# Convolution of prompt tiles 1 to 3 moved from VectorE to ScalarE and TensorE, with consumers of gathers queued later and 80 value rows fetched ahead

## Chip, cores and metric

The kernel runs on one core of a Trainium2 chip. The metric is the device time of one execution in microseconds (us), as the median of several runs. Times in the text that are places (such as "from 433 to 519") count from the start of the profiled span.

## What is computed

One layer of a hybrid decoder step: 512 prompt tokens in four tiles of 128, and 32 sample tokens (8 sequences of 4). Per token: a projection of x to 5192 columns, a gated causal depthwise convolution of width 31 over 512 channels, attention over keys that an indexer selects, a gated merge with an output product and layer norm, and then a product-key mixture of experts, in which each token takes 128 rows of a table `peer_u` and 128 rows of a table `peer_v` (16384 rows of 1024 floats each). Cut to what matters:

```python
u, q, k, v, qi, ki, wi, g_conv, g_attn = project_inputs(x, pos, w_in)   # u = a * sigmoid(b)
full = concatenate([prev, u])                                           # 30 rows of the past, then u
y = sum(full[n + k] * conv_w[k] for k in range(31)) + conv_b            # per channel, 512 channels
conv = silu(layer_norm(y)) @ w_conv_out
o = sparse_attend(q, k, v, select_keys(indexer_scores(qi, wi, ki), topk=128))
m = sigmoid(g_conv) * conv + sigmoid(g_attn) * o
h = layer_norm(ALPHA * x + m @ w_out)
idx, g = product_key_top16_of_8_heads(h @ w_query)                      # 128 experts per token
a = gelu(sum(h * peer_u[idx], -1)) * g
y = layer_norm(ALPHA * h + sum(a * peer_v[idx]))
```

Everything is float32.

## The kernel before

There are five tiles: 0 to 3 of the prompt, 4 for the samples. Each goes through a **front** (projection rows in, rotation, index scores, top-k, attention, convolution, merge, output product, layer norm, queries, routing) and then through the **mixer**: 128 gathers of u rows (tile 4: 32), each 128 partitions by 1024 floats (512 KB), each dotted with h on VectorE (L1908); Gelu and gates; then one gather of v rows per token (128, or 32 for tile 4), whose product with the weights TensorE sums into `acc` (L1552, in pairs; ScalarE first writes the weights of four tokens into a column, L1138). All gathers are issued by GpSimd (L800) in one list, `FETCHES`, which `fetches()` writes (L383 to L403). They land in `rings`: 5 slots for u, 6 for v. A gather waits until its slot is free, which is when the dot (semaphore `dotted`) or the product (`summed`) of the row before it in that slot is done. The first u gather of a tile also waits for the tile's first routed head (`routed`, L1716), and so on every 16.

The order of work on each engine is fixed when the program is built. Every piece of a front yields a number; the tables `CLOCK_0`, `CLOCK_1` and `CLOCK_T` turn it into a time of a planner's clock, fetches and their consumers have such times too (`fetches`, `uses`), and `merge` writes each engine's instructions in order of these times. So the clock only sets an order; on the chip, each engine goes through its own list and stops at each wait. Tile 0's u gathers stand at 176 and on, its first 64 v gathers (`EARLY_V`) at 470 and on, and from `MIXED_FROM` = 600 there are steps of 358.4 of the clock: step t holds the u gathers of tile t, the remaining v gathers of tile t-1 (first 24 u with two v each, then the rest spread), and the first 32 v of tile t. The consumer of a gather stands `LANDING` = 8 after it (14 for the first 32 v rows). The front of tile t+1 stands 103 after the start of step t.

The convolution works on `uT` (L113), the transposed gated rows with 30 columns of the past ahead. `taps` (L1730 to L1747) runs it on VectorE: for each of the 31 taps, four operations (one for each 128 channels) add a shifted view times the tap's weight into `conv_acc`. In tiles 1 to 3 it is merged with `attention` (L1806), between 0.195 and 0.475; attention itself runs from AT_ATT = 0.20 to AT_TAIL = 0.48, ahead of it the top-k from 0.09. An attention group is one or two heads: scores on TensorE (L1386), row maximum on VectorE (L1761), exp on ScalarE (L975), transposes on TensorE (L1403), their copy on ScalarE (L990), P·V on TensorE (L1415) into `wide`, heads 0 to 7 in its first bank and 8 to 15 in its second. Tile 1 has 8 groups, tiles 2 and 3 have 16. Then TensorE transposes the convolution's result after `conv_done` (L1261), ScalarE applies Silu (L929), and the products follow (L1243, queries L1304).

`wide` is free from the output product of the tile before until the first P·V; for tile 1, it is in use by the projection of all later tiles until `z_copied_b` has its last count.

## Time and profile before

| | us |
|---|---|
| median of 3 runs | 2325.19 (2320.65 to 2331.3) |
| profiled execution | 2312.72 |
| its span | 2310.9 |
| PE / DVE / ACT / POOL busy | 1513.1 / 1463.2 / 286.4 / 1251.1 |
| mean granted clock of TensorE | 0.789 |
| moved by DMA | 683.98 MB, 296 GB/s over the span |

A float32 product shows as two MATMUL records, a dot as two DVE records (the operation and the read of its accumulator). No engine is busy throughout, so the stretches have to be read one by one.

### The profile page before, as it was taken

How to read it: one execution, taken by the hardware profiler on the slowest of the kernel's cores; microseconds unless marked ns; L12 is line 12 of the kernel's file. 1: busy time of each engine (PE TensorE's matmuls, PEld its weight loads, DVE VectorE, ACT ScalarE, POOL GpSimd, SP SyncE). 2: the span in 40 equal slices, each digit the busy share in tenths (PEclk: the TensorE clock that was granted, in tenths of full speed). 3: DMA queues.
4: the chain of work that ended last, by engine and by line, in shares of the span. 5: the costliest groups of instructions: out<-in, count | busy, mean ns of one | idle time of the engine just before them, and what ended most of it. 6: DMA issues, size and time to landing. Idle time of an engine off the chain costs nothing.

```text
span 2310.9 us, 19606 instructions
## 1 busy us (share of the span) xinstructions
PE 1513.1 (65%) x6002; PEld 619.2 (27%) x6002; DVE 1463.2 (63%) x3807; ACT 286.4 (12%) x713; POOL 1251.1 (54%) x1108
## 2 busy tenths in 40 slices
PE   7889999268755356685546787556832887584244
PEld 3454444232411123231112334111100333141011
DVE  4319956971297899738589965776799641138431
ACT  1411102120101112010111211011100121000000
POOL 1003455654377667647677865777655644233654
PEclk9999999569977655798876878887555789777668
DMA  8807999868589888879998998999977999656996
GB/s 314 319 24 282 323 381 332 270 223 285 200 320 375 312 273 305 315 256 364 365 354 301 327 352 286 358 346 328 358 262 247 330 339 323 247 161 224 296 325 239
DMA packets 215683, 683.98 MB, mean 296 GB/s; under 512 B 27637, under 2 KB 63061, under 8 KB 208979
## 3 DMA queue, kind: packets, MB, share of 16 engines
q0 software_dynamic: 157376, 581.67, 71.0%
q1 hardware_dynamic: 51195, 91.90, 11.5%
q10 hardware_dynamic: 7008, 9.17, 1.1%
q8 instruction: 48, 0.79, 0.1%
q14 instruction: 56, 0.46, 0.1%
HBM read 669.97 MB, written 13.10 MB: 296 GB/s over the span
## 4 chain that ended last, share of the span: by engine, by line
DVE 31%; PE 28%; DMA 16%; POOL 13%; issue 8%; ACT 2%; SPq 2%; POOLq 0%; DVEq 0%; ACTq 0%
POOL rings L800 13%; DVE rings L1908 10%; PE acc L1552 9%; DMA rings<-peer_v,late 9%; DMA rings<-peer_u,late 5%; PE wide L1243 4%; DVE conv_acc L1744 3%; PE bank L1304 3%; DVE small L1616 2%; DVE uah L1619 2%; PE acc L1192 2%; DVE soft_score L1619 1%; PE wide L1464 1%; PE acc L1225 1%; PE bank L1456 1%
## 5 line engine op out<-in xcount | busy, mean ns | idle before, releaser
L1552 PE MATMUL acc<-rings,z_stages 128*32 128x512 f32 x2048 | 614.9, 757 | 499.7 <-DMA rings<-peer_v,late 303.1
L800 POOL DMA_INDIRECT rings<-peer_u,late x544 | 650.8, 1196 | 513.0 <-DVE late L1908 274.7
L800 POOL DMA_INDIRECT rings<-peer_v,late x544 | 591.6, 1088 | 446.9 <-PE acc L1552 295.9
L1908 DVE CUSTOM_DVE_ANT_0 rings<-rings,uah 128x1024 f32<-128x1024 f32 x288 | 348.9, 1223 | 149.5 <-DMA rings<-peer_u,late 145.4
L1908 DVE CUSTOM_DVE_ANT_0 rings<-rings,late 128x1024 f32<-128x1024 f32 x256 | 310.2, 1222 | 93.2 <-DMA rings<-peer_u,late 89.3
L1552 PEld LDWEIGHTS acc<-rings,z_stages 128*32 128x32 f32 x2048 | 126.4, 126 | 900.6 <-issue 897.1
L1225 PE MATMUL acc<-rings 128*128 128x512 f32 (+1 forms) x352 | 149.9, 578 | 0.0
L1744 DVE SCALAR_TENSOR_TENSOR conv_acc<-uah,conv_p,conv_acc 128x128 f32<-128x128 f32 x480 | 133.1, 347 | 0.0
L1678 DVE MAX8 uah<-zt 128x8 f32<-128x128 f32 (+1 forms) x80 | 22.7, 284 | 142.1 <-ACT zt L958 142.1
L1415 PE MATMUL wide<-keep,soft_score 128*128 128x64 f32 x320 | 62.0, 353 | 67.4 <-ACT soft_score L990 67.4
L1138 ACT COPY z_stages<-late 128x4 f32<-128x4 f32 x136 | 26.2, 198 | 574.7 <-PE acc L1552 507.7
L1304 PEld LDWEIGHTS bank<-uah,w_query_s 128*128 128x128 f32 x640 | 82.4, 210 | 25.1 <-issue 22.0
L1304 PE MATMUL bank<-uah,w_query_s 128*128 128x128 f32 (+1 forms) x640 | 87.2, 297 | 2.3 <-ACT uah L947 2.3
L1415 PEld LDWEIGHTS wide<-keep,soft_score 128*128 128x128 f32 x320 | 55.0, 258 | 104.3 <-ACT soft_score L990 96.9
L1225 PEld LDWEIGHTS acc<-rings 128*128 128x128 f32 x352 | 63.5, 193 | 71.2 <-issue 70.9
L1243 PE MATMUL wide<-w_out_s,uah 128*128 128x512 f32 (+1 forms) x160 | 79.0, 645 | 2.1 <-ACT uah L940 2.1
L1192 PE MATMUL acc<-rings 128*128 128x512 f32 (+2 forms) x176 | 69.2, 541 | 15.1 <-DMA small<-quarter 12.6
L1225 PE MATMUL wide<-rings,uah 128*128 128x512 f32 (+1 forms) x176 | 74.4, 565 | 0.0
L975 ACT ACTIVATE soft_score<-soft_score,small 128x128 f32<-128x128 f32 (+3 forms) x64 | 35.6, 557 | 286.0 <-DVE small L1766 286.0
L1403 PE MATMUL bank<-ident_s,soft_score 128*128 128x128 f32 x160 | 34.4, 349 | 44.4 <-ACT soft_score L975 44.4
L1386 PE MATMUL bank<-keep,queries 64*128 64x128 f32 (+3 forms) x128 | 57.4, 599 | 3.9 <-ACT soft_score L1031 3.9
L1243 PE MATMUL wide<-w_conv_out_s,conv_acc 128*128 128x512 f32 (+1 forms) x80 | 46.9, 728 | 4.4 <-ACT conv_acc L929 4.4
(232 smaller groups left out, 1623.4 us busy)
## 6 DMA issues: line engine op xcount, KB each, us to landing
rings<-w_in SPq DMA_DIRECT2D x36, 1024.0 KB, 7.7
rings<-peer_u,late POOLq DMA_INDIRECT x544, 6.2
rings<-peer_v,late POOLq DMA_INDIRECT x544, 6.1
w_query_s<-cache_kT SPq DMA_DIRECT2D x64, 128.0 KB, 6.1
w_query_s<-cache_v SPq DMA_DIRECT2D x64, 128.0 KB
z_rows<-z_stages ACTq DMA_DIRECT2D x30, 256.0 KB, 6.9
soft_score<-ln SPq DMA_DIRECT2D x6, 1024.0 KB, 10.7
zt<-z_rows SPq DMA_DIRECT2D x2, 2596.0 KB, 12.0
```

The costliest lines, as they stand in the source:

```text
L800: nc.gpsimd.indirect_dma_start(ring[:, place, :], None, table, offs).then_inc(done[place], 16)
L1192: last = nc.tensor.matmul(acc[:, i % 2 * BLK + lo:i % 2 * BLK + hi], xT_0[:, k, :], w[:, c, :], start=(k == 0), stop=(k == KC - 1))
L1225: last = nc.tensor.matmul(z_bank[j][:, 0:width], x[j][:, m, :], w[:, c, :], **flags)
L1243: last = nc.tensor.matmul(dst[0:n, half * BLK:(half + 1) * BLK], lhs[:, c, 0:n], rhs[:, c, half * BLK:(half + 1) * BLK], start=(c == 0), s ...
L1304: last = nc.tensor.matmul(s_bank[r][:, h * P:h * P + n], wqu[:, c, col:col + PEER_DQ], aT3[:, c, 0:n], start=(c == 0), stop=(c == KC - 1))
L1386: last = nc.tensor.matmul(s_bank[g % 2][:, k * seen:(k + 1) * seen], qT3[half_rows[h % 2], h // 2, :], kT3[half_rows[h % 2], h // (N_HEADS ...
L1415: last = nc.tensor.matmul(wide[:, o * HEAD_DIM:(o + 1) * HEAD_DIM], pt2[:, g % 2, at * P:(at + 1) * P], v3[:, j, kv * HEAD_DIM:(kv + 1) * ...
L1552: last = nc.tensor.matmul(acc_v[QUAD * j:QUAD * (j + 1), half * BLK:(half + 1) * BLK], lone[:, quad % LONE, j, QUAD - 1 - m:2 * QUAD - 1 - m],
L1616: chain.link(V.max(top, values))
L1619: chain.link(V.match_replace(values, top, values, TAKEN))
L1744: ins = V.scalar_tensor_tensor(ca3[:, c, :], src, cp[:, c, k:k + 1], ca3[:, c, :], ALU.mult, ALU.add)
L1908: V.tensor_tensor_reduce(out=u_ring[:, place, :], in0=u_ring[:, place, :], in1=h, scale=1.0, scalar=0.0, op0=ALU.mult, op1=ALU.add, accum_ ...
```

## The change

In tiles 1 to 3 the convolution no longer runs on VectorE. Each tap is two steps, one for each half of the 512 channels. In a step ScalarE copies two shifted 128x128 views scaled by the tap's weight into a buffer of 256 columns (two buffers, in unused columns of `score` and `bias` for tile 1, in the second half of `z_stages` for tiles 2 and 3), and TensorE multiplies the buffer by the identity and accumulates in the second bank of `wide`. ScalarE may be two steps ahead. After step 62 ScalarE adds the bias on the way to `conv_T3` (which shares columns with the index queries) and signals `conv_done`. P·V of heads 8 to 15 now waits for that. The steps stand between 0.19 and 0.325 in tile 1, between 0.055 and 0.31 in tiles 2 and 3. Tile 0 and the samples keep their convolution on VectorE.

Besides, the planner's numbers change: tile 0 has 80 early v gathers instead of 64, 1.4 apart instead of 1.7; the steps start at 590 instead of 600; within the steps a consumer stands 13 after its gather instead of 8 (14 for the first 32 v rows, as before); tile 1's front has a shorter clock from 0.2 on; and the final norm of tile 2 stands 3.5 later. Moving code into `rectified`, `index_products` and `attention` on TensorE changes nothing by itself.

```diff
+    conv_T3 = queries[:, 1024:1536].rearrange("p (c n) -> p c n", c=CC)
+    stage_1 = z_stages[:, BLK:2 * BLK]
+    SCALED = CC // 2 * P
+    scaled_of = [None, (score[:, SCALED:], bias[:, SCALED:])] + [(stage_1[:, 0:SCALED], stage_1[:, SCALED:])] * (N_TILES - 2)
...
-    MIXED_FROM, SLOT_US, LANDING = 600.0, 1.4, 8.0
-    EARLY_V, SLOW_U = (HALF, P // 4, P // 4, P // 4), 24
+    MIXED_FROM, SLOT_US, LANDING, LANDING_MIXED = 590.0, 1.4, 8.0, 13.0
+    EARLY_V, SLOW_U = (5 * P // 8, P // 4, P // 4, P // 4), 24
...
-            yield 470.0 + 1.7 * i, ("v", 0, i)
+            yield 470.0 + 1.4 * i, ("v", 0, i)
...
-            yield at + LANDING + (6.0 if table == "v" and number < HALF // 2 else 0.0), table, tile, number
+            mixed = step_at(1) <= at < step_at(N_TILES)
+            weights_first = table == "v" and number < HALF // 2
+            yield at + (LANDING_MIXED + weights_first if mixed else LANDING + 6.0 * weights_first), table, tile, number
...
-    CLOCK_1 = ((0.0, 328.0), (0.012, 345.0), (0.02, 348.0), (0.05, 360.0), (0.09, 374.0), (0.2, 410.0), (0.48, 500.0),
+    CLOCK_1 = ((0.0, 328.0), (0.012, 345.0), (0.02, 348.0), (0.05, 360.0), (0.09, 374.0), (0.2, 408.0), (0.48, 480.0),
...
+    def tap_at(t, step):
+
+        lo, hi = (0.19, 0.325) if t == 1 else (0.055, 0.31)
+        return lo + (hi - lo) * step / (2 * CONV_W)
...
+        def scaled_taps(t):
+
+            before = steps_before(t)
+            for step in range(2 * CONV_W):
+                k, half = step // 2, step % 2
+                yield tap_at(t, step)
+                if step == 0:
+                    act.wait_ge(t_copied, groups_before(t) + GROUPS)
+                if before + step >= 2:
+                    act.wait_ge(tap_added, before + step - 1)
+                for j in range(2):
+                    c = 2 * half + j
+                    last = nc.scalar.activation(scaled_of[t][half][:, j * P:(j + 1) * P], uT3[:, c, k:k + P], ACT.Copy,
+                                                scale=cp[:, c, k:k + 1])
+                last.then_inc(tap_scaled, 1)
+            yield tap_at(t, 2 * CONV_W) + 0.005
+            act.wait_ge(tap_added, before + 2 * CONV_W)
+            act.wait_ge(idx_mm, idx_before(t + 1))
+            for c in range(CC):
+                last = nc.scalar.activation(conv_T3[:, c, :], wide[:, BLK + c * P:BLK + (c + 1) * P], ACT.Identity,
+                                            bias=cp[:, c, CONV_W:CONV_W + 1])
+            last.then_inc(conv_done, 1)
...
+        def added_taps(t):
+
+            before = steps_before(t)
+            for step in range(2 * CONV_W):
+                k, half = step // 2, step % 2
+                yield tap_at(t, step) + 0.002
+                if step == 0:
+                    if t == 1:
+                        pe.wait_ge(z_copied_b, N_TARGETS * (N_BLK + 1))
+                    else:
+                        pe.wait_ge(h_ready, t)
+                pe.wait_ge(tap_scaled, before + step + 1)
+                nc.tensor.matmul(wide[:, BLK + half * SCALED:BLK + (half + 1) * SCALED], ident[:, :], scaled_of[t][half],
+                                 start=(step == 0), stop=(k == CONV_W - 1), skip_group_check=True).then_inc(tap_added, 1)
...
                 pe.wait_ge(p_copied, before + g + 1)
+                if t and g == n_groups // 2:
+                    pe.wait_ge(conv_done, t + 1)
...
-                yield from merge(taps(t, AT_ATT - 0.005, AT_TAIL - 0.005), attention(t, AT_ATT, AT_TAIL))
-            V.nop().then_inc(conv_done, 1)
+                yield from attention(t, AT_ATT, AT_TAIL)
```

What stands in the queues at three places follows. GpSimd, the gathers at the end of tile 0's u rows and the start of step 1. Before:

```order
L800 DMA rings<-peer_u,late 128x1024 x128
L835 MEMSET z_stages 128x512
L800 DMA rings<-peer_v,late 128x1024 x64
L800 DMA rings<-peer_u,late 128x1024
L800 DMA rings<-peer_v,late 128x1024 x2
```

GpSimd at the same place in the changed kernel:

```order
L814 DMA rings<-peer_u,late 128x1024 x128
L849 MEMSET z_stages 128x512
L814 DMA rings<-peer_v,late 128x1024 x80
L814 DMA rings<-peer_u,late 128x1024
L814 DMA rings<-peer_v,late 128x1024 x2
```

Sixteen v gathers moved ahead of the first u gather of tile 1. After 24 such pairs of one u and two v, before there were six u and one v sixteen times, now 104 u rows follow in a run; both end with the 32 early v rows of tile 1.

TensorE, tile 1's attention, from the first transposes to the second group's (bank0 to bank3 are PSUM banks; soft_score holds exp's results and, for tile 1, the scaled taps). Before:

```order
L1403 MATMUL bank2<-ident_s,soft_score 128x128 [waits exped,z_copied_b,v_kept]
L1403 MATMUL bank2<-ident_s,soft_score 128x128 x3
L1386 MATMUL bank0<-keep,queries 128x256 [waits maxed]
L1386 MATMUL bank0<-keep,queries 128x256
L1415 MATMUL wide<-keep,soft_score 128x64 [waits p_copied]
L1415 MATMUL wide<-keep,soft_score 128x64 x3
L1403 MATMUL bank3<-ident_s,soft_score 128x128 [waits exped]
```

TensorE at the same place in the changed kernel, from the last tap products ahead of the first transposes:

```order
L1370 MATMUL wide<-soft_score,ident_s 128x256 [waits tap_scaled] x6
L1470 MATMUL bank2<-ident_s,soft_score 128x128 [waits exped]
L1470 MATMUL bank2<-ident_s,soft_score 128x128 x3
L1453 MATMUL bank0<-keep,queries 128x256 [waits maxed]
L1453 MATMUL bank0<-keep,queries 128x256
L1370 MATMUL wide<-soft_score,ident_s 128x256 [waits tap_scaled] x4
L1484 MATMUL wide<-keep,soft_score 128x64 [waits p_copied]
L1484 MATMUL wide<-keep,soft_score 128x64 x3
L1370 MATMUL wide<-soft_score,ident_s 128x256 [waits tap_scaled] x12
L1470 MATMUL bank3<-ident_s,soft_score 128x128 [waits exped]
```

About 16 tap products stand in each of the groups 0 to 3, each with a wait for ScalarE. On ScalarE five steps stand ahead of the first exp and 57 behind it. In the last two groups of this attention stood, before, the first v rows of tile 0; now they stand after the attention.

VectorE, tile 2's attention, from its first row maximum to the second (L1908 and L1975 are dots, L1761 and L1828 row maxima). Before:

```order
L1761 ISA soft_score,small<-bank0,soft_score 128x384 [waits qk_mm]
L1761 ISA small 128x1
L1766 TENSOR_SCALAR small<-small 128x1 [waits dve_chain2]
L1908 ISA rings,late<-rings,uah 128x1024 [waits u_in1]
L1908 ISA late 128x1
L1740 TENSOR_SCALAR conv_acc<-uah,conv_p 128x128 [waits t_copied]
L1740 TENSOR_SCALAR conv_acc<-uah,conv_p 128x128 x3
L1908 ISA rings,late<-rings,uah 128x1024 [waits u_in2]
L1908 ISA late 128x1
L1744 SCALAR_TENSOR_TENSOR conv_acc<-uah,conv_p,conv_acc 128x128 [waits dve_chain2] x4
L1761 ISA soft_score,small<-bank1,soft_score 128x384 [waits qk_mm]
```

VectorE at the same place in the changed kernel:

```order
L1828 ISA soft_score,small<-bank0,soft_score 128x384 [waits qk_mm]
L1828 ISA small 128x1
L1833 TENSOR_SCALAR small<-small 128x1 [waits dve_chain2]
L1975 ISA rings,late<-rings,uah 128x1024 [waits u_in4]
L1975 ISA late 128x1
L1975 ISA rings,late<-rings,uah 128x1024 [waits u_in0]
L1975 ISA late 128x1
L1975 ISA rings,late<-rings,uah 128x1024 [waits u_in1]
L1975 ISA late 128x1
L1975 ISA rings,late<-rings,uah 128x1024 [waits u_in2]
L1975 ISA late 128x1
L1828 ISA soft_score,small<-bank1,soft_score 128x384 [waits qk_mm]
```

The taps are gone, and between two row maxima there are now about three dots, where there were about three dots and eight taps' operations.

## Rows read from the trace of the kernel before

**Rows 1.** Busy time per stretch: start:end, length, engines, PEclk, DMA share, GB/s.

```profile
433.00:519.00 86.00, 46.74 (x169) 28.16 (x169) 71.73 (x222) 19.64 (x50) 49.45 (x39) 0.58 0.69 227
519.00:611.00 92.00, 78.42 (x340) 29.78 (x339) 13.17 (x19) 10.34 (x27) 46.22 (x48) 0.94 0.83 287
611.00:638.00 27.00, 14.83 (x109) 9.71 (x107) 8.42 (x33) 2.83 (x7) 0.94 (x1) 0.87 0.18 72
638.00:725.00 87.00, 47.17 (x142) 9.80 (x144) 80.09 (x275) 2.67 (x8) 68.50 (x60) 0.74 0.93 339
...
774.00:814.00 40.00, 7.20 (x16) 1.27 (x16) 38.90 (x85) 0.00 (x0) 24.54 (x23) 0.54 0.87 292
814.00:914.00 100.00, 63.94 (x204) 34.21 (x205) 99.20 (x271) 18.95 (x50) 71.93 (x55) 0.59 0.86 288
914.00:1026.00 112.00, 77.22 (x343) 40.55 (x342) 62.56 (x121) 14.27 (x32) 59.83 (x55) 0.82 0.81 284
...
1230.00:1334.00 104.00, 78.12 (x304) 37.03 (x304) 95.99 (x261) 23.22 (x55) 82.64 (x65) 0.75 0.91 315
```

The columns between the length and PEclk are busy us and number of instructions of PE, PEld, DVE, ACT and POOL; POOL's are the gathers.

**Rows 2.** POOL in order of time, first u gather of tile 1: idle before it.

```profile
638.51 0.94 POOL L800 DMA_INDIRECT rings<-peer_u,late  x1 [26.57 <-DVE late L1716]
```

**Rows 3.** Page, costliest groups (busy us, mean ns | idle before, releaser) and landing times.

```profile
L800 POOL DMA_INDIRECT rings<-peer_u,late x544 | 650.8, 1196 | 513.0 <-DVE late L1908 274.7
...
L1908 DVE CUSTOM_DVE_ANT_0 rings<-rings,uah 128x1024 f32<-128x1024 f32 x288 | 348.9, 1223 | 149.5 <-DMA rings<-peer_u,late 145.4
...
L1744 DVE SCALAR_TENSOR_TENSOR conv_acc<-uah,conv_p,conv_acc 128x128 f32<-128x128 f32 x480 | 133.1, 347 | 0.0
...
L1138 ACT COPY z_stages<-late 128x4 f32<-128x4 f32 x136 | 26.2, 198 | 574.7 <-PE acc L1552 507.7
...
rings<-peer_u,late POOLq DMA_INDIRECT x544, 6.2
```

**Rows 4.** DVE in order of time, tile 2's attention: start, us, what.

```profile
819.79 1.22 DVE L1908 CUSTOM_DVE_ANT_0 rings<-rings,uah 128x1024 f32<-128x1024 f32 x1
...
820.93 1.14 DVE L1744 SCALAR_TENSOR_TENSOR conv_acc<-uah,conv_p,conv_acc 128x128 f32<-128x128 f32 x4
821.98 0.55 DVE L1761 CUSTOM_DVE_ANT_0 soft_score<-bank,soft_score 128x384 f32<-128x384 f32 x1
```

**Rows 5.** ACT in order of time, tile 2's Silu: four operations together.

```profile
920.52 1.50 ACT L929 ACTIVATE conv_acc<-bank,conv_p 128x128 f32<-128x128 f32 x4 [0.86 <-PE bank L1267]
```

**Rows 6.** Chain that ended last, samples' attention: start, us, what (two records per product).

```profile
1857.58 6.98 PE wide L1509 x18
...
1905.38 1.91 PE acc L1552 x8
...
1918.57 4.28 PE wide L1509 x18
```

**Rows 7.** Busy time per stretch, v rows (L1552) alone: PE, PEld, PEclk, DMA.

```profile
433.00:519.00 86.00, 10.33 (x40) 2.16 (x40) 0.58 0.69 227
519.00:611.00 92.00, 43.92 (x192) 9.97 (x192) 0.94 0.83 287
```

**Rows 8.** All engines in order of time, one group of tile 1's attention.

```profile
444.56 0.51 ACT L975 ACTIVATE soft_score<-soft_score,small 128x256 f32<-128x256 f32 x1 [9.81 <-DVE small L1766]
...
445.56 0.56 ACT L990 COPY soft_score<-bank 128x512 f32<-128x512 f32 x1
...
446.18 1.97 PE L1415 MATMUL wide<-keep,soft_score 128*128 128x64 f32 x8 [8.19 <-ACT soft_score L990]
...
447.94 1.06 PE L1403 MATMUL bank<-ident_s,soft_score 128*128 128x128 f32 x4
...
448.93 2.07 PE L1386 MATMUL bank<-keep,queries 64*128 64x256 f32 x4
```

**Rows 9.** Busy time per stretch, u dots (L1908) alone: DVE, PEclk, DMA.

```profile
774.00:814.00 40.00, 20.97 (x36) 0.54 0.87 292
814.00:914.00 100.00, 58.51 (x97) 0.59 0.86 288
```

More of the change, by code:

```diff
@@ L1023, in front @@
                 keep_values(t)
[L1025 to L1033 removed]
+                yield from merge(itertools.chain(rectified(t), attention(t, AT_ATT, AT_TAIL)), scaled_taps(t))
                 if t == 1:
@@ L1038, in front, with rectified @@
             yield from tail(t, P)
+        def rectified(t):
+            seen, per = (t + 1) * P, heads_per_group(t, IDX_HEADS)
+            for g in range(IDX_HEADS // per):
+                yield AT_IDX + 0.005 * per * g + 0.001
+                act.wait_ge(idx_mm, idx_before(t) + g + 1)
+                if g >= 2:
+                    act.wait_ge(idx_used, (t - 1) * IDX_HEADS + per * (g - 1))
+                nc.scalar.activation(sc2[:, g % 2, 0:per * seen], s_bank[g % 2][:, 0:per * seen],
+                                     ACT.Relu).then_inc(idx_relu, 1)
         def front_sample():
@@ L1343, in front @@
                     transpose_group(t_bank[g], pairs(Z_Q + 4 * P * g, 4), P, P)
-                yield 0.33
-                pe.wait_ge(t_copied, 5)
-                lo, hi = 0.34, 0.47
+                yield from attention(t, 0.33, 0.34, 0.47)
             else:
@@ L1363, in front, with attention @@
                 transpose_group(t_bank[1], pairs(Z_A, CC), P, P)
-                per_idx = heads_per_group(t, IDX_HEADS)
-                for g in range(IDX_HEADS // per_idx):
-                    yield AT_IDX + 0.005 * per_idx * g
-                    if g >= 2:
-                        pe.wait_ge(idx_relu, idx_before(t) + g - 1)
-                    for k in range(per_idx):
-                        h = head_of(g, k, per_idx)
-                        last = nc.tensor.matmul(s_bank[g % 2][:, k * seen:(k + 1) * seen],
-                                                qiT3[half_rows[h % 2], h // 2, :], kiT[half_rows[h % 2], 0:seen],
-                                                start=True, stop=True)
-                    last.then_inc(idx_mm, 1)
-                yield AT_TOPK
-                pe.wait_ge(t_copied, first + GROUPS)
+                yield from merge(itertools.chain(index_products(t), attention(t, AT_TOPK, AT_ATT, AT_TAIL)), added_taps(t))
+            yield from conv(t, P)
+            yield from tail(t, P)
+        def attention(t, at, lo, hi):
+            before = att_before(t)
+            half_rows = [slice(HEAD_DIM * r, HEAD_DIM * (r + 1)) for r in range(2)]
+            seen, per = (t + 1) * P, heads_per_group(t, N_HEADS)
+            n_groups = N_HEADS // per
+            yield at
+            if t == 0:
+                pe.wait_ge(t_copied, 5)
+            else:
+                pe.wait_ge(t_copied, groups_before(t) + GROUPS)
                 pe.wait_ge(idx_relu, idx_before(t + 1))
-                lo, hi = AT_ATT, AT_TAIL
             step = (hi - lo) / n_groups
@@ L1418, in front @@
                 last.then_inc(pv_mm, 1)
-            yield from conv(t, P)
-            yield from tail(t, P)
         def front_sample():
```

41 lines of the change are left out of this document (23 added, 18 removed), and 6 rows, old and new, of the table CLOCK_1.

## The prediction

> **What bounds the kernel now.** I read the page first, then the busy time per stretch, then who waits for whom. From about 180 us on, GpSimd (POOL) issues 1088 gathers of 512 KB, one expert row for each of 128 tokens: the u rows, which VectorE (DVE) dots with h, and the v rows, which TensorE (PE) weights and sums. Everything else is the fronts of the tiles (projection rows in, top-k, attention, convolution, products, routing), and they stand in the same in-order queues. So two things can bound: the gathers' own pace, or a front on which the next gathers wait. The stretches of [rows 1] tell which; in each row the reader is to look at the DVE and PE busy time against the length, and at the DMA share.
>
> 433 to 519 is tile 1's attention together with its taps: DVE is busy 71.7 of 86 us, DMA only 0.69. 519 to 611 is tile 1's tail (convolution product, output product, query product) with v rows of tile 0: PE is busy 78.4 of 92. 611 to 638 is a hole: DMA at 0.18, one gather. It ends when POOL's first gather of u rows of tile 1 starts at 638.51, after 26.57 us of waiting for the first routed head of tile 1 [rows 2]; all 64 early v rows had been issued. 638 to 725 is routing beside gathers, DMA 0.93. 774 to 814 is tile 2's top-k, DVE 38.9 of 40. 814 to 914 is tile 2's attention with taps: DVE busy 99.2 of 100, the bound without a doubt, DMA down to 0.86. 1230 to 1334, the same for tile 3: DVE 96.0 of 104, but DMA 0.91 and PE 78.1. In the page, POOL waited 274.7 us in all for DVE's dots before u gathers [rows 3].
>
> So DVE is the bound in two of the three attentions, nearly so in the third, and the front of tile 1 opens a hole of 27 us that is worth its whole length.
>
> **What comes off DVE.** Per tile 1 to 3, 4 tap operations for each of 31 taps: 120 at 347 ns besides the first four [rows 3]; 133.1 us for four tiles is 33.3 per tile. Tile 0 keeps its own. From start to start a group of four takes 1.05 us and a dot 1.14 [rows 4], so 31 groups free 32 to 34 us of DVE per tile.
>
> **What goes onto ScalarE and PE.** 62 steps per tile; a step is two ScalarE operations of 128x128 and one PE product of 128x256 by the identity. The trace has neither in this form. The nearest ScalarE row is the four 128x128 activations of tile 2's Silu, 1.50 us, or 0.375 each [rows 5]: 0.75 a step, 46.5 a tile. They have a scale and a bias by pointer, the tap has a scale alone, so this is the upper side. The lower side is its 128x4 copy at 198 ns [rows 3], 0.40 a step, which has hardly any columns. I take 0.75, by the row of the same shape. The nearest PE rows are nine 128x256 products in 6.98 us and in 4.28 us [rows 6]: 0.776 or 0.476 a step, 29 to 48 us a tile. Two buffers let ScalarE be two steps ahead, so a step costs the longer of the two, plus what of the hand-off isn't hidden: 0.75 to 0.8.
>
> The row on ScalarE shows 0.375 us for an operation with two pointer operands. The Trainium skill, ScalarE: Activation LUTs, What ACT_TABLE_LOAD costs, gives 186 ns plus 0.833 ns a column, 93 ns for each pointer operand, and an overlap of 93 ns back to back. For two pointers that is 0.386, with which the trace agrees. For one it is 0.293, so by it the step would be an estimated 0.59 and the tile 36 us instead of 46.5; the sum below would gain some 10 us.
>
> **Where the taps stand.** In tiles 2 and 3, 35 of the 62 steps stand ahead of the first exp, in a top-k where PE has 7.2 us of work in 40 and ScalarE none [rows 1]. Those I cost at nothing; what hides them is DVE's top-k, and without it they would cost 35 times 0.75, 26 us. The other 27 stand between attention groups 0 to 6 of 16. In tile 1 only five steps stand ahead of the first exp: ScalarE then waits in order for the first row maximum, and PE behind it. The other 57 lie in groups 0 to 3 of 8. Behind a waiting tap product on PE stand the scores, transposes and P·V products of the next groups, in tiles 2 and 3 v rows also, and for those wait POOL's v gathers. The new wait for conv_done before the second half of the heads stands after the last step and costs nothing beyond it.
>
> **Tile 1's attention, 86 us.** DVE falls to 71.7 - 33.3 = 38.4. ScalarE rises to 19.6 + 57 x 0.75 = 62. PE loses ten v rows (40 records, four to a row, 10.3 us [rows 7]), which now come after the attention, and gains 57 x 0.476 to 0.776: 46.7 - 10.3 + 27 to 44 = 63 to 80. A group at the low clock of this stretch (0.58) is 1.97 + 1.06 + 2.07 = 5.1 us of PE and about 1.6 of ScalarE [rows 8]. The stage ends between 64 and 86; I take 76, **-10**.
>
> **Tile 1's tail, to 638.** The ten rows come here, at 1.91 us a pair [rows 6]: 9.6 us of PE, where it had 92 - 78.4 = 13.6 idle. I take **+8**. The first head is then routed at about 636. Meanwhile 80 v rows instead of 64 are issued. About 63 are done on PE when the query product ends, 15 us earlier; eleven more free the ring for the 80th, at some 1.4 us each. So the rows end where the routing ends, and the hole of 27 us is filled by 16 gathers that step 1 need no longer make. That gain is counted below.
>
> **Step 1 (638 to 1035), 397 us.** It has 208 gathers instead of 224, 104 of them u rows in a run. The front of tile 2 stands a fixed time behind the step's start, so at gather 52 instead of 59. Routing stretch: 8 gathers fewer, but DVE is busy 80.1 of 87, so **-10**. The load, rotation and index products (725 to 774) are a chain of latencies: 0. Top-k: it held 18 dots (36 records, two to a dot [rows 9]) in 22 gathers, now some 23 in 23, so 5 x 1.14, **+6**. Attention: 48 dots and 34 us of taps in 100. Without taps DVE has 65. The next limit is the u ring: five slots, 6.2 us to landing [rows 3], 1.22 for the dot and 0.3 to the next issue, 7.7 for five, 1.55 a gather; 49 gathers take 76. Four steps of taps in each of the early groups add some on PE: 82, **-18**. Tail (914 to 1026): fewer v rows, PE 77 of 112, **-5**. Sum -27.
>
> **Steps 2 and 3.** Tile 3's attention: 65 gathers in 104 us. At 1.45, the pace of 638 to 725, they need 94. PE goes from 78.1 to 78.1 + 27 x 0.476 to 0.776 = 91 to 99. I take 101, **-3**. The rest keeps its DVE work: 0.
>
> **Consumers 5 us later.** In the queues a dot or v row stands behind 5 us more of front work. This can help, since DVE waited 145.4 us for landings of u rows before these dots [rows 3], with front work behind it. It can hurt, since a ring slot is freed later, and POOL already waits 274.7 us for dots. Both are shifts by three or four gathers per step, not sums: -8 to +8, taken at 0.
>
> **Sum.** -10 + 8 - 27 - 3 = -32. The profiled execution took 2312.72 us (span 2310.9 and 1.8 around it), so it would be 2281; the median of the three runs lies 12.5 higher, 2325.19, and by it I forecast **2293**.
>
> **Rivals.** (a) *The taps vanish.* PE's granted clock is 0.54 in the top-k and 0.58 and 0.59 in the attentions, where it waits, but 0.94 in the dense tail [rows 1]. If tap products lift it to the upper level (2.4 GHz), steps cost 0.476 and a group's own work nearly halves. Then tile 1's attention is 64 (-22), tile 2's 76 (-24), its tail -10, tile 3's 95 (-9); with +8, -10 and +6 this is -61: **2264**. For it speaks the tail; against it, that in 1230 to 1334 PE was busy 75% and still had 0.75. The Trainium skill, TensorE: Matmul & The Clock Gate, What's actually happening, says that activity releases the throttle; [rows 1] agree in direction.
>
> (b) *No change that can be measured.* Tile 1's attention stays at 86 (PE at the low clock, each group waiting in turn for taps), the tail takes all 10, tile 2's attention falls only to 95, tile 3's rises by 4: 0 + 10 - 10 + 6 - 5 - 5 + 4 = 0, **2325**. The 16 gathers would be ahead, but the front of tile 2 sets the end of step 1, and they are worth little.
>
> (c) *Slower: the taps become the chain.* In the attentions nothing hides a step of s us, and groups and taps add up: tile 1, 57 s + 8 x 6 against 86; tile 2, 27 s + 16 x 4.0 (PE records of a group at the low clock) against 100; tile 3, 27 s + 78 against 104; fixed, +8 - 10 + 6 - 5 = -1. In all 111 s - 101. It turns at s = 0.91 us. At 0.75 it is -18; if each hand-off between ScalarE and PE costs so much that a step takes 1.2, it is +32, **2357**. Against it: two buffers, and part of every step lies beside waits that groups have anyway.
>
> (d) That the convolution of tiles 1 to 3 isn't moved at all is excluded: the order of DVE has no tap rows there.
>
> **How the numbers follow.** Forecast 0.50 (2275 to 2310), (a) 0.18, (b) 0.17, (c) 0.15. The measurement can tell about 0.5%, so faster means below 2313.6: 0.50 + 0.18 + 0.02 of (b) = 0.70. Same: 0.15 of (b) and 0.01 of (c), 0.16. Slower: 0.14. The range 2258 to 2335 holds (a), the forecast, (b) and the near side of (c).
>
> **What would show it.** Taps: 31 groups of four gone from DVE in each attention; tap products on PE of 0.48 to 0.78 us and pairs of activations of 0.6 to 0.75. Tile 1's attention 76 us long, with DVE below half. No wait of POOL for routing above 10 us before the first u gather of tile 1, which starts at 636 give or take 8. Tile 2's attention 82 us with DVE at 80%. The first u gather of tile 2 near 1006 instead of 1035. I am wrong if tile 1's attention is as long as before or longer with PE waiting for ScalarE's taps, if the hole stays, or if the pace outside the attentions changes by over 8 us in a step.

## The result, and the profile after

The changed kernel takes **2342.92 us** (median of 5 runs, 2336.75 to 2353.79), where the kernel before takes 2325.19: a ratio of **1.0072**, 95% interval 1.0048 to 1.0097, so it is slower, by 0.5 to 1.0%. Forecast were 2293 us, 2258 to 2335; the sign was wrong too. The profiled execution took 2353.79 us, the slowest of its five, and that of before 2312.72, below the fastest of its own five (2320.65): the two profiles differ by 41 us, the medians by 17.7. So I read from the traces where time moves, and take the size from the ratios.

Busy time per stretch of the changed kernel, columns as in [rows 1] (length; PE, PEld, DVE, ACT, POOL; PEclk, DMA share, GB/s):

```profile
433.00:503.00 70.00, 57.51 (x235) 36.41 (x236) 38.99 (x92) 53.68 (x159) 40.29 (x31) 0.91 0.67 227
503.00:611.00 108.00, 95.63 (x368) 33.17 (x368) 13.36 (x19) 11.97 (x31) 51.86 (x55) 0.91 0.80 271
611.00:646.00 35.00, 28.48 (x176) 14.05 (x172) 8.67 (x35) 3.69 (x11) 17.99 (x20) 0.94 0.84 295
646.00:731.00 85.00, 41.78 (x144) 9.42 (x146) 80.22 (x275) 3.17 (x11) 57.75 (x52) 0.80 0.94 346
781.00:822.00 41.00, 16.52 (x52) 7.44 (x51) 39.94 (x86) 17.33 (x51) 21.24 (x20) 0.76 0.77 245
822.00:914.00 92.00, 67.19 (x228) 43.70 (x228) 74.17 (x156) 36.32 (x105) 69.76 (x53) 0.61 0.86 291
...
1226.00:1327.00 101.00, 82.49 (x355) 40.67 (x356) 68.40 (x142) 43.14 (x117) 77.48 (x66) 0.89 0.93 334
```

Tile 1's attention (first row) is 70 us where it was 86, DVE down to 39.0. The hole is gone: DMA is at 0.84 in the third row where it was at 0.18. But the tail of tile 1 (second and third row) is 143 us where it was 119. The routing stretch (646 to 731) has 52 gathers where it had 60 and is 85 us where it was 87, with the same 275 instructions on DVE. Tile 2's attention is 92 us where it was 100, with DVE at 74.2.

GpSimd in order of time, first u gather of tile 1, against 638.51 and a wait of 26.57 in [rows 2]:

```profile
646.23 0.94 POOL L814 DMA_INDIRECT rings<-peer_u,late  x1 [2.44 <-DVE late L1783]
```

The page's groups, against [rows 3]:

```profile
L814 POOL DMA_INDIRECT rings<-peer_u,late x544 | 630.9, 1160 | 538.8 <-DVE late L1975 329.9
...
L1975 DVE CUSTOM_DVE_ANT_0 rings<-rings,uah 128x1024 f32<-128x1024 f32 x288 | 349.3, 1223 | 155.0 <-DMA rings<-peer_u,late 150.5
...
L1370 PE MATMUL wide<-z_stages,ident_s 128*128 128x256 f32 x248 | 87.0, 460 | 44.9 <-ACT z_stages L960 44.8
...
L960 ACT ACTIVATE z_stages<-uah,conv_p 128x128 f32<-128x128 f32 x248 | 82.0, 392 | 50.1 <-PE wide L1370 49.8
```

POOL now waits 329.9 us for dots instead of 274.7, though 100 us of taps have left DVE. That row was the one to explain. Its sum is no measure of the time by itself: in e5 below, 25 us faster than before, it is 311.8.

### The profile page after: what moved, and what is told of

It is laid out like the page before. It is cut to its first block, busy times and chain, and to the rows that moved or that the text cites. A ratio compares the mean times of both kernels' runs of the same rounds, so it can differ in the third digit from the quotient of the medians.

```text
span 2352.0 us, 20364 instructions
## 1 busy us (share of the span) xinstructions
PE 1611.4 (69%) x6374; PEld 673.3 (29%) x6374; DVE 1371.3 (58%) x3435; ACT 407.7 (17%) x1097; POOL 1228.0 (52%) x1108
## 4 chain that ended last, share of the span: by engine, by line
PE 32%; DVE 28%; DMA 17%; POOL 11%; issue 7%; ACT 3%; SPq 2%; POOLq 0%; DVEq 0%; ACTq 0%
PE acc L1619 11%; POOL rings L814 10%; DMA rings<-peer_v,late 9%; DVE rings L1975 8%; DMA rings<-peer_u,late 6%; PE wide L1283 3%; PE bank L1345 3%; DVE small L1683 3%; PE wide L1370 2%; DVE uah L1686 2%; PE acc L1232 2%; DVE soft_score L1686 1%; DVE conv_acc L1811 1%; PE wide L1576 1%; PE acc L1265 1%
## 5 line engine op out<-in xcount | busy, mean ns | idle before, releaser
L1619 PE MATMUL acc<-rings,z_stages 128*32 128x512 f32 x2048 | 606.3, 747 | 448.7 <-DMA rings<-peer_v,late 274.2
L814 POOL DMA_INDIRECT rings<-peer_u,late x544 | 630.9, 1160 | 538.8 <-DVE late L1975 329.9
L1975 DVE CUSTOM_DVE_ANT_0 rings<-rings,uah 128x1024 f32<-128x1024 f32 x288 | 349.3, 1223 | 155.0 <-DMA rings<-peer_u,late 150.5
L1975 DVE CUSTOM_DVE_ANT_0 rings<-rings,late 128x1024 f32<-128x1024 f32 x256 | 309.4, 1224 | 108.2 <-DMA rings<-peer_u,late 104.4
L1178 ACT COPY z_stages<-late 128x4 f32<-128x4 f32 x136 | 26.0, 198 | 584.9 <-PE acc L1619 519.2
L1370 PE MATMUL wide<-z_stages,ident_s 128*128 128x256 f32 x248 | 87.0, 460 | 44.9 <-ACT z_stages L960 44.8
L960 ACT ACTIVATE z_stages<-uah,conv_p 128x128 f32<-128x128 f32 x248 | 82.0, 392 | 50.1 <-PE wide L1370 49.8
L1484 PE MATMUL wide<-keep,soft_score 128*128 128x64 f32 x320 | 54.4, 323 | 24.8 <-ACT soft_score L1027 24.8
L1370 PEld LDWEIGHTS wide<-z_stages,ident_s 128*128 128x128 f32 x248 | 43.1, 209 | 98.6 <-ACT z_stages L960 70.6
L1370 PE MATMUL wide<-soft_score,ident_s 128*128 128x256 f32 x124 | 42.2, 455 | 25.6 <-ACT soft_score L960 25.2
```

The lines of the kernel that those rows point to most:

```text
L814: nc.gpsimd.indirect_dma_start(ring[:, place, :], None, table, offs).then_inc(done[place], 16)
L960: last = nc.scalar.activation(scaled_of[t][half][:, j * P:(j + 1) * P], uT3[:, c, k:k + P], ACT.Copy, scale=cp[:, c, k:k + 1])
L1370: nc.tensor.matmul(wide[:, BLK + half * SCALED:BLK + (half + 1) * SCALED], ident[:, :], scaled_of[t][half], start=(step == 0), stop=(k == ...
L1484: last = nc.tensor.matmul(wide[:, o * HEAD_DIM:(o + 1) * HEAD_DIM], pt2[:, g % 2, at * P:(at + 1) * P], v3[:, j, kv * HEAD_DIM:(kv + 1) * ...
L1619: last = nc.tensor.matmul(acc_v[QUAD * j:QUAD * (j + 1), half * BLK:(half + 1) * BLK], lone[:, quad % LONE, j, QUAD - 1 - m:2 * QUAD - 1 - m],
L1975: V.tensor_tensor_reduce(out=u_ring[:, place, :], in0=u_ring[:, place, :], in1=h, scale=1.0, scalar=0.0, op0=ALU.mult, op1=ALU.add, accum_ ...
```

## The experiments

Eighteen kernels ran; each ratio is against runs of the kernel before on the same chip, whose median was 2325.0 to 2341.4 us by chip. "Best" is the kernel of e5.

| | ratio (95% interval) |
|---|---|
| e1 convolution moved, alone | 0.9956 (0.9926 to 0.9986) |
| e2 consumers 13 behind their gathers, alone | 1.0104 (1.0053 to 1.0154) |
| e3 80 early rows, alone | 1.0051 (1.0021 to 1.0081) |
| e4 changed kernel with consumers at 8 | 0.9987 (0.9955 to 1.0019) |
| **e5 the same with 64 rows, 1.7 apart: best** | **0.9891 (0.9856 to 0.9927)** |
| e6 changed kernel, 13 in step 3 only | 1.0036 (1.0014 to 1.0059) |
| e7 changed kernel, 13 for dots only | 1.0106 (1.0070 to 1.0142) |
| e8 changed kernel, 13 for v rows only | 1.0006 (0.9981 to 1.0031) |
| e9 best, 48 early rows | 0.9900 (0.9870 to 0.9931) |
| e10 best, dots 5 behind | 0.9887 (0.9849 to 0.9924) |
| e11 best, 80 rows, 16 of them last | 0.9944 (0.9914 to 0.9975) |
| e12 best, 2 of 31 taps | 0.9816 (0.9779 to 0.9853) |
| e13 changed kernel with 64 rows | 1.0051 (1.0020 to 1.0083) |
| e14 best, fronts at 93 | 1.0031 (1.0005 to 1.0058) |
| e15 e11, fronts at 93 | 1.0060 (1.0027 to 1.0092) |
| e16 before, tile 1's new clock alone | 0.9951 (0.9921 to 0.9981) |
| e17 e13, fronts at 108 | 0.9946 (0.9924 to 0.9968) |
| e18 best, fronts at 113 | 0.9977 (0.9953 to 1.0001) |

**The parts apart.** e1 is the changed kernel with all planner numbers of before, e2 and e3 are the kernel before with one edit each (e2 with the final norm of tile 2 3.5 later too, as in the changed kernel), e4 is the changed kernel with `LANDING` for every consumer. Of e1's edit against the changed kernel (the second pair is e4's too):

```diff
-    EARLY_V, SLOW_U = (5 * P // 8, P // 4, P // 4, P // 4), 24
+    EARLY_V, SLOW_U = (HALF, P // 4, P // 4, P // 4), 24
...
-            yield at + (LANDING_MIXED + weights_first if mixed else LANDING + 6.0 * weights_first), table, tile, number
+            yield at + LANDING + (6.0 if table == "v" and number < HALF // 2 else 0.0), table, tile, number
```

> Only the convolution moves; every number of the planner is that of before (64 early rows, steps from 600, consumers 8 after their gathers, tile 1's old clock). Theory L (the taps pay a little, the later consumers cost more): 2310 to 2320, 5 to 15 below before, and the third step (first u gather of tile 3 to first v gather of tile 3) at 417 as before. Rival T (the taps themselves are what costs, through waits between ScalarE and TensorE): 2335 or more. If the tile-1 front alone decides, the first u gather of tile 1 comes at about 625 instead of 638.

> The kernel before with one change: within the steps a consumer stands 13 after its gather instead of 8 (and the final norm of tile 2 stands 3.5 later, which this needs). Theory L: slower by 10 to 25 us, most of it in step 3 and behind it. Rival T: within 5 us of before.

> The kernel before with 80 early v rows, 1.4 apart, instead of 64, 1.7 apart. Theory L: 0 to 5 us faster; the hole before the first u gather of tile 1 shrinks from 27 us to under 10, but TensorE is denser in the front of tile 1, so that gather comes 3 to 8 us later than 638, and step 1 is no more than 10 us shorter. By the prediction's sum the filled hole would be worth 10 us or more.

> The changed kernel with consumers 8 after their gathers again (14 for the first 32 v rows), all else as changed. Theory L: 10 to 25 us faster than the changed kernel, 2318 to 2333, by step 3 and the tail. Rival T: 2340 as the changed kernel.

The move alone gains 0.44%, so the taps as such aren't what went wrong. The later consumers cost 1.0% alone (e2) and 0.85% inside the changed kernel (e4 against 1.0072). The 80 rows cost 0.5% alone (e3), where my theory had a gain of up to 5 us: the first u gather of tile 1 comes at 662.5 there, 24 us later than before, and step 1 is only 3 us shorter.

**The rows and tile 1's clock.** e5 takes 64 rows at 1.7 and keeps the new clock; e16 puts that clock alone (with the steps from 590) into the kernel before; e9 has 48 rows; e11 has 80, the last 16 behind the rest. e11 against e5, besides the number of rows:

```diff
-            yield 470.0 + 1.7 * i, ("v", 0, i)
+            yield 470.0 + 1.7 * min(i, HALF) + 0.7 * max(i - HALF, 0), ("v", 0, i)
```

> The convolution moved, with the new clock of tile 1's front and the steps from 590, but 64 early rows at 1.7, and consumers 8 behind their gathers. It differs from the kernel with the convolution alone (2317.5 us) by that clock alone, and from the changed kernel with consumers at 8 (2320.2 us) by the 16 rows alone. Theory 'hole' (the gap of about 27 us before the first u gather of tile 1 is worth its length, so rows that fill it pay): the hole stays, the attention of tile 1 ends near 503 us instead of 521, the first u gather near 625 us instead of 640.7, time about 2310. Theory 'chain' (step 1 is bound by the front of tile 2, and rows put ahead only lengthen the tail of tile 1 on TensorE): the same gain of 15 us at the first u gather, and it stays to the end, since fewer v rows then stand beside the tail: about 2302. No change against the convolution alone: 2317.

> The kernel before with the new clock of tile 1's front and the steps from 590 alone, the convolution on VectorE. With the convolution moved, that clock gave 15 us (ratio 0.9956 to 0.989), since v rows no longer stand inside tile 1's attention. If the gain belongs to the order of TensorE alone: about 0.993 here as well. If it needs VectorE free of the taps (busy 71.7 of 86 us in that attention): no gain, 0.998 to 1.003.

> The best kernel so far (convolution moved, new clock of tile 1, consumers 8, 64 early rows at 1.7: ratio 0.989) with 48 early rows instead of 64, so sixteen v rows more stand in step 1. Theory 'chain' (every v row that TensorE sums ahead of tile 1's routing delays the front by its 1.2 to 1.4 us, and step 1 has room for it): the first u gather of tile 1 some 12 us earlier, time 8 to 15 us shorter, ratio about 0.984. Rival 'pace' (now the hole before the routing is larger, and step 1 is bound by the number of its gathers): 5 to 15 us longer, ratio about 0.994.

> The same base with 80 early rows, 64 of them at 1.7 as before, and the last 16 at 0.7, so that their sums stand beside or behind tile 1's query product. With 1.4 for all 80 they stood ahead of it, and cost 22 us (ratio 0.9987 against 0.989). Theory 'chain': the price of the 80 rows was their place ahead of the output and query products; here the query product ends at 607 as in the base, the rows fill part of the hole, and the first u gather is at most 12 us later: ratio 0.987 to 0.993. Rival 'count': what costs is that the list holds 80 rows ahead of the first u gather, wherever their sums stand: ratio about 0.998.

e5 is about 25 us under before (median 2304.16 against 2329.98); e9 and e10 can't be told from it. Against e4 it gains 0.96%, 22 us. That agrees better with the "chain" theory (18 us) than with the other (10 us). The expectation calls the 16 rows the only difference, but there are three: the rows, their spacing (1.7 instead of 1.4) and the final norm of tile 2, 3.5 earlier. e11 keeps e5's spacing and norm and loses 0.53%, 12 us, with the 16 rows; the other 10 us belong to the spacing and the norm, which no run parts (each of these differences is known to some 0.5% only). In what follows "the 16 rows" of e4 are all three. v rows on TensorE (L1617 there) ahead of tile 1's routing, columns PE, PEld, PEclk, DMA, GB/s. e5, from the attention's end to the layer norm, to the end of the query product, to the first u gather:

```profile
503.00:561.00 58.00, 27.73 (x120) 5.90 (x120) 0.96 0.76 260
561.00:608.00 47.00, 25.55 (x106) 5.60 (x104) 0.96 0.85 297
608.00:623.00 15.00, 7.95 (x32) 1.96 (x32) 0.91 0.54 188
```

e4, the same three:

```profile
507.00:580.00 73.00, 38.19 (x156) 8.09 (x158) 0.94 0.80 276
580.00:634.00 54.00, 29.79 (x118) 6.50 (x114) 0.94 0.85 291
634.00:649.00 15.00, 6.21 (x30) 1.55 (x32) 0.89 0.70 244
```

At four records a row, e4 has 9 rows more in the first and 3 more in the second stretch: 14.7 us more of PE, and the stretches are 15 and 7 us longer. At 1.4 apart the rows stand ahead of products that they stood behind at 1.7. In e11 these two stretches are as in e5 (layer norm at 561 to 562, query product done at 607), but the first u gather still stands behind the 16 rows. First u gather of tile 1 in e5, then in e11:

```profile
622.79 0.94 POOL L812 DMA_INDIRECT rings<-peer_u,late  x1 [7.42 <-DVE late L1781]
```

```profile
641.01 0.94 POOL L812 DMA_INDIRECT rings<-peer_u,late  x1 [0.30 <-issue]
```

So the hole was no room to fill: with the new clock it is 7.42 us, 64 rows fill the rest, and 16 more move the first u gather by 18 us (e11) or 26 (e4). From it to the first u gather of tile 2 take 387 us in e5, 378 in e11, 377 in e4: the 16 rows are worth 9 or 10 us to step 1, half of what they cost there. With 48 rows that u gather comes at 617.5 and step 1 takes 401 us, and the time is the same: between 48 and 64 it is flat, which neither of e9's theories had.

e16 shows what the clock alone does. Its attention of tile 1, still with all taps on DVE:

```profile
433.00:503.00 70.00, 32.10 (x110) 23.95 (x108) 69.38 (x214) 13.92 (x39) 46.94 (x31) 0.50 0.72 225
```

The attention ends at 505.5, 13 us earlier than before (518.8), though DVE is busy 69.4 of 70; in e1, with the taps moved and the old clock, it ends at 521. From the mask of the top-k to the end of the last P·V, so without what shifts its start, it takes 86.6 us before, 86.2 in e1, 76.0 in e16 and 73.9 in e5. So it was shortened by taking tile 0's v rows out of it; taking the taps off DVE alone did nothing there, and 2 us once the rows were gone. Both together give 0.9891; the product of e1 and e16 would be 0.9907, the same within the intervals.

**Where the later consumers cost.** One edit each in `uses`:

```diff
-            mixed = step_at(1) <= at < step_at(N_TILES)
+            mixed = table == "u" and step_at(1) <= at < step_at(N_TILES)
```

> The changed kernel with the consumers 13 behind their gathers in step 3 alone (the sample front and its neighbours), 8 in steps 1 and 2. Between 2320.2 us (8 everywhere) and 2342.9 us (13 everywhere). Theory 'sample front' (the later place hurts where the front of the samples and the end of tile 3 stand in step 3): about 2340. Rival 'every step pays alike': a third of 22.7 us, about 2328.

> The changed kernel with 13 for the u dots on VectorE alone, and 8 for the v rows on TensorE. Theory 'dots' (the u ring's slots come free later, behind more of VectorE's front work): nearly the whole cost, about 2340. Rival 'rows' (it is the v rows on TensorE): about 2322.

> The changed kernel with 13 for the v rows on TensorE alone, and 8 for the u dots on VectorE. Theory 'dots': nearly no cost, about 2322. Rival 'rows' (TensorE's rows stand behind front products that themselves wait, and the front's next products behind the rows): about 2340. If both this and its twin come to 2330 or so, the two parts add up; if both stay near 2320, only the pair costs, by the order in which the two rings come free.

> The same base, with the u dots 5 behind their gathers in the steps instead of 8. Putting them at 13 had cost 27 us (ratio 1.0106 against 0.9987). If a dot that stands behind a waiting piece of a front is what keeps ring slots occupied, then 5 takes more of them ahead of such pieces: 5 to 12 us shorter, ratio about 0.986. Rival: at 5 (less than the 6.2 us that a row needs to land) VectorE comes to the dot before the row is there, and the front behind it waits: 5 to 15 us longer, ratio about 0.993.

It is the place of the dots: 1.2% with 13 for them alone, 0.2% for the v rows alone (both against e4). Step 3 alone gives 0.5% of the 0.85% of all steps, between the two theories of e6. The parts don't add up exactly (1.2% for the dots is more than 0.85% for both), but the intervals overlap. At 5 instead of 8 nothing changes that can be told. One place in e7 shows what happens, where the front of the samples begins. ScalarE waits 28 us for rows that come back from DRAM (`zt<-choose`). e7:

```profile
1594.39 0.20 ACT L1178 COPY z_stages<-late 128x4 f32<-128x4 f32 x1 [28.12 <-DMA zt<-choose]
...
1594.73 3.75 PE L1619 MATMUL acc<-rings,z_stages 128*32 128x512 f32 x16 [15.99 <-ACT z_stages L1178]
...
1598.60 0.94 POOL L814 DMA_INDIRECT rings<-peer_v,late  x1 [9.57 <-PE acc L1619]
...
1602.13 0.23 DVE L1896 TENSOR_SCALAR soft_score<-zt,small 32x32 f32<-32x32 f32 x1 [12.54 <-ACTq L1101]
...
1605.24 1.69 POOL L814 DMA_INDIRECT rings<-peer_u,late  x1 [4.46 <-DVE late L1975]
```

e4, the same place:

```profile
1580.49 0.20 ACT L1176 COPY z_stages<-late 128x4 f32<-128x4 f32 x1 [28.17 <-DMA zt<-choose]
...
1582.86 3.63 PE L1617 MATMUL acc<-rings,z_stages 128*32 128x512 f32 x8
...
1583.60 0.33 DVE L1894 TENSOR_SCALAR soft_score<-zt,small 32x32 f32<-32x32 f32 x1 [2.12 <-ACTq L1099]
...
1586.71 1.69 POOL L812 DMA_INDIRECT rings<-peer_u,late  x1 [2.79 <-DVE late L1973]
```

ScalarE waits as long in both. In e4 DVE passes that time with dots, which stand ahead of the front's piece, and waits 2.12 us; in e7 they stand behind it, it waits 12.54, and POOL's next wait for a dot is 4.46 us where it is 2.79. POOL's longer stop there, 9.57, isn't for a dot but for the v ring: the v rows stand at 8 in both kernels, but ScalarE writes their weights (L1178) only behind the piece that waits for DRAM, and TensorE waits 15.99 for them. Over the whole span POOL's waits grow from 321.3 to 338.5 us for dots and from 317.5 to 337.2 for sums of v rows, so about half of the added waiting is at the other ring; how it gets there, no run took apart. From a u gather's start to the end of its dot, over tile 3's 128 rows, e7 has a median of 10.95 us against 11.56 in e4, but a 90th percentile of 21.2 against 17.2 (for tile 1's rows 17.3 against 13.8). In tile 3 the typical row is used sooner and the late ones later, and a ring that is used in order stops at a late one.

**The place of the front.** If the harm is that front pieces stand ahead of landed rows, then a front that is put earlier must do it too, and moving the front along with the consumers must undo it.

```diff
-    FRONT_LAG, FINISH_LAG, LN2_LAG = 103.0, 318.0, 20.0
+    FRONT_LAG, FINISH_LAG, LN2_LAG = 108.0, 318.0, 20.0
```

> The changed kernel with 64 early rows at 1.7 (consumers 13, new clock, convolution moved). It completes a square: 64 rows and consumers 8 gave 0.989, 80 and 8 0.9987, 80 and 13 1.0072. If the two prices add: 0.9975, about 2323 us. If the later consumers only cost with the 80 rows: 0.990. If the rows only cost with consumers at 8 too: 1.006.

> The best kernel (ratio 0.989) with the fronts of tiles 2, 3 and of the samples 93 behind the start of their step instead of 103, so about six gathers earlier. Theory 'front binds the step': each step is up to 6 us shorter, 5 to 15 us in all, ratio about 0.985. Rival 'balanced': the front then collides with the routing stretch before it, where VectorE is busy 90% and DMA 0.98: no change or longer, ratio 0.989 to 0.996.

> 80 early rows with the last 16 behind the query product (ratio 0.9944), and the fronts at 93. Theory 'front binds the step': with 16 gathers fewer in step 1 the earlier front can use the room, ratio about 0.988, a gain over 0.9944 that is larger than the gain of the fronts at 93 with 64 rows. Rival: the 16 rows never pay: ratio 0.994 or above.

> The kernel with 64 early rows and consumers at 13 (ratio 1.0051), with the fronts of tiles 2, 3 and of the samples 5 later as well (108 behind the step's start), so that they stand against the dots and sums as in the best kernel (0.989), and only the gathers are 5 earlier against both. Reading A (the place against the front): back to 0.989 to 0.994. Reading B (the distance from gather to consumer): stays at 1.002 to 1.007.

> The best kernel with the fronts of tiles 2, 3 and of the samples 113 behind the step's start instead of 103; at 93 the ratio was 1.0031. If the place has an optimum that is narrow: 0.998 to 1.005. If only a front that comes too early costs (consumers stall behind it), while a later one has room: 0.986 to 0.992. Dots at 5 instead of 8 did nothing (0.9887), which speaks for the second.

e14 and e15 refute my theory that the front only needs to come earlier: 10 earlier costs 33 us with 64 rows and 27 with 80. e13 refutes that the prices add: with 64 rows the later consumers cost 1.6%, 37 us, not 20, and with the later consumers the 16 rows cost only 0.2%, within the noise. And e17 takes back 24 of these 37. POOL's waits for dots in the whole span (sum, times, longest), e5, e13, e17 (for sums of v rows it waits 302.3, 307.3 and 321.2):

```profile
POOL rings L812 <- DVE late L1973: 311.8, 161, 10.9
```

```profile
POOL rings L814 <- DVE late L1975: 345.7, 160, 12.1
```

```profile
POOL rings L814 <- DVE late L1975: 310.2, 160, 11.2
```

And the stretch of tile 3's first 64 u gathers, again e5, e13, e17:

```profile
1434.00:1655.00 221.00, 144.35 (x414) 32.86 (x410) 157.09 (x479) 21.18 (x65) 155.31 (x135) 0.73 0.98 347
```

```profile
1461.00:1700.00 239.00, 144.75 (x416) 32.91 (x412) 159.35 (x480) 21.13 (x64) 161.56 (x134) 0.71 0.92 319
```

```profile
1444.00:1667.00 223.00, 145.26 (x406) 32.66 (x402) 158.08 (x485) 21.00 (x64) 158.06 (x134) 0.72 0.97 341
```

The same gathers (134 or 135 records on POOL) and nearly the same DVE work take 18 us more in e13, with DMA at 0.92 instead of 0.98, and e17 has it back. So the place of the dots against the front is the larger part of the cause; the 13 us that e17 doesn't give back, and why the price is 37 us with 64 rows and 20 with 80, stay open. Of the 13 us, about 5 are there at tile 1's first u gather (627.8 against 622.8) and 7 in step 1 (393.8 against 387.0). e18 does the same instructions in another order that leaves wrong rows in y, so its time is only a sign: a front 10 later costs 0.9% too. "Landed rows behind a front piece" doesn't explain that side, so as far as e18 counts, the place has an optimum near 103 that this argument gives only in part.

**The taps' price.** e12 has 2 of the 31 taps in tiles 1 to 3 and leaves 29 out; the same replacement is made in `tap_at` and wherever steps are counted.

```diff
-            for step in range(2 * CONV_W):
+            for step in range(2 * N_TAPS):
```

> The same base with 2 of the 31 taps in tiles 1 to 3 (29 taps of the convolution are left out, 58 of the 62 steps). It measures what the moved taps still cost on ScalarE and TensorE. If they still lie on the chain in tile 1's attention (75 us long now) and at the start of tile 2's and 3's: 15 to 30 us shorter, ratio about 0.980. If the waits of the groups hide them: within 5 us of the base, 0.989.

0.9816 against 0.9891: the moved taps still cost some 17 us. In the traces, from the mask of the top-k to the last P·V, tile 1's attention takes 63 us in e12 and 74 in e5, tile 2's 88 and 89, tile 3's 96 and 99: of the attentions, tile 1's pays, where the taps can't start in the top-k. But that isn't all of it. The first u gather of tile 1 comes 8 us sooner in e12, step 1 is 4 us shorter (383.0 against 387.0) and step 2 is 11 (413.6 against 424.6), of which 7 lie ahead of the mask of tile 3's top-k, where the prediction put the taps at nothing. Both traces are single, and the two profiles differ by 27 us, more than the 17 of the ratios.

## Why the prediction was wrong

**What held.** DVE as the bound of tile 2's and tile 3's attentions before, the fall of DVE (39.0 us in tile 1's attention, where 38.4 was forecast), and the step's price. In tile 1's attention DVE wasn't the bound: e1 takes the taps off and it is as long as before; what e1 gains, it gains in step 1 (396 to 385 us from first u gather to first u gather) and step 2 (420 to 412). ScalarE and PE in order of time, changed kernel, tile 2's top-k and tile 1's attention:

```profile
786.94 1.28 ACT L960 ACTIVATE z_stages<-uah,conv_p 128x128 f32<-128x128 f32 x4 [0.20 <-PE wide L1370]
788.42 1.28 ACT L960 ACTIVATE z_stages<-uah,conv_p 128x128 f32<-128x128 f32 x4 [0.20 <-PE wide L1370]
```

```profile
439.58 5.12 PE L1370 MATMUL wide<-soft_score,ident_s 128*128 128x256 f32 x14
```

Two steps take 1.48 us from start to start, 0.74 each, where 0.75 was forecast. The four activations take 1.28; at a mean of 392 ns each on the page, that is an overlap, and (1.28 - 0.39) / 3 is 0.30 us from one to the next. That agrees with the estimate of 0.293 from the figures of the Trainium skill (ScalarE: Activation LUTs, What ACT_TABLE_LOAD costs). It didn't make the step 0.59, because every second step adds a 0.20 us wait for PE, and the activation behind the wait takes its full 0.39. The PE row gives 0.73 a product (14 records, 7 products, in 5.12 us), but that is the pace that ScalarE sets and not PE's own price. Rival (c), which turned at 0.91 us, is refuted by e1: the move gains. Rival (a) is refuted as the outcome, though its clock came true in tile 1 (below).

**The step that failed first: the 16 rows.** "The hole of 27 us is filled by 16 gathers that step 1 need no longer make", and a tail of tile 1 of +8. The tail took 24 more, and the 16 rows cost 22 us in all with consumers at 8 (e4 against e5; 12 of them with e5's spacing, e11). I had counted the ten rows that left the attention, and not that 80 rows at 1.4 put 12 more rows ahead of the query product than 64 at 1.7 do (e4 against e5). The hole also counted twice: the earlier end of the attention already closes it from the front's side, down to 7.42 us in e5.

**The second: what 16 gathers fewer are worth.** Step 1 was to shrink by 27 us; in the traces it shrinks from 396 to 387: the taps alone give 11 (385 in e1; 387 with the new clock, e5), the rows 9 or 10, and the later consumers take 10 back (377 in e4). "Routing stretch: 8 gathers fewer, -10" was -2: six of the eight were v rows, DVE has 17 dots there in both kernels, and that stretch is bound by DVE, which has the same 275 instructions as before [rows 1] and 80.2 of 85 us busy. Tile 2's attention was to be 82 us and is 92, though DVE is at 74.2 of 92. The step that failed is the one from "DVE has 65" to "the next limit is the u ring": from the top-k's mask to the last P·V the stretch takes 89 us in e5 and 88 in e12 with hardly a tap, so the taps don't set it, and DVE, 69.6 of 88 us busy in e12, isn't full. Its groups, with PE mostly at the low clock (0.61), are what is left; no run took them apart.

**The third: "Consumers 5 us later: -8 to +8, taken at 0".** The measured price is 20 us within the changed kernel, 24 alone, 37 with 64 rows. The mistake was to weigh the two arguments as equals. The help was small: DVE's wait for landings in the row of [rows 3] is 145.4 us before and 134.4 with nothing but the later consumers (e2), and in the changed kernel it is 150.5 against 145.9 in e4, so it didn't fall at all. A wait for a landing is short (150.5 us over 288 dots, 0.5 each); a front piece that waits for another engine or for DRAM held what stood behind it for 12.54 us at the place shown.

**The sum, with what was measured.** Move and tile 1's clock: -25 us (e5); 80 rows: +22 (e4 against e5); consumers: +20 (changed kernel against e4); together +17, the measured 17.7 but for rounding, as differences of the same four ratios must. The split depends on the order in which the edits are taken: with 64 rows the consumers cost 37 and the rows then 5 (e13), so of these 42 us only the sum is firm. The forecast was -32 for all. The convolution and the clock with their 25 us came near it in size, but for a reason that holds in part only: e1 and e16 show that the old order of TensorE, with v rows inside tile 1's attention, was worth as much (-0.49%) as DVE's taps (-0.44%). Rival (b) came nearest on the rows ("they are worth little"), but none had the rows or the consumers at a cost; the slower one blamed the taps.

## What to carry to other kernels

Before work is put into a hole, ask which queue closes the hole: a row fetched ahead is also a product in front of the front, and here 16 of them moved the next u gather by twice what they were worth later. A number that shifts consumers against a front isn't a fine adjustment: count at each long wait of the front (here 28 us for DRAM) how many landed rows stand behind it. And when several numbers change with an idea, cost each one by itself, and in pairs: the idea gained 0.4%, with tile 1's clock 1.1%, and the rows and the later consumers lost 1.8%.

## What the runs showed of the hardware

Tap products raise TensorE's granted clock in one attention and hardly in another. In tile 1's attention, stretches of 10 us from 443 to 483 show 1.00 (2.4 GHz) in the changed kernel and in e5, and 0.50 (1.2 GHz) in the kernel before; over the attention it is 0.91 against 0.50 in e16, with PE busy 57.5 of 70 us against 32.1. In e12, without most taps, it is 0.50 again (433 to 490, PE busy 34.3 of 57), so it is the taps that raise it. In tile 2's top-k the tap products alone also have 1.00 (786 to 799, PE busy 11.2 of 13), yet in the attention behind it the mean stays at 0.61, with PE busy 67.2 of 92. e12's attention of tile 1 is still 11 us shorter, at the lower clock: the clock gives back less than the taps take.
